# Half of the output weights split in the output phase, and two of the gated attention's four token factors made from the other two

## The reference

```
b = cumsum(log_a) within a chunk of 64 tokens
b_last = b[last of chunk];  b_ref = b[middle of chunk]
att = (q * exp(b - b_ref)) @ (k * exp(b_ref - b)).T, causal within the chunk
o_intra = att @ v
q_inter = q * exp(b)
k_state = k * exp(b_last - b)
decay   = exp(b_last)
for each chunk: o_inter = q_inter @ state; state = decay * state + k_state.T @ v
o = rms_norm(o_intra + o_inter) * silu(gate)
x = x + concat([o, cross_attention]) @ w_out
```

## Time and profile before

| what | value |
|---|---|
| median of 3 runs | 2726.78 us (2722.53 to 2730.62) |
| the profiled execution: its time | 2718.5 us |
| the profiled execution: its span | 2716.7 us |
| mean granted clock of TensorE | 0.979 |
| busy: PE, weight loads, DVE, ACT, POOL | 96%, 81%, 49%, 31%, 7% |
| `gla_phase` | 220 to 424 us of the span |
| first output phase | 427 to 548 us of the span |

### The profile page before, as it was taken

How to read it: one execution, slowest core, us unless ns; L and a number is a source line. 1 busy time by engine, 2 the same in 40 slices (tenths; PEclk the granted TensorE clock), 3 DMA queues, 4 the chain that set the end, 5 groups by cost and what they waited for, 6 DMA issues and landing times. The chain is left out here.

```text
span 2716.7 us, 33074 instructions
## 1 busy us (share of the span) xinstructions
PE 2596.6 (96%) x12444; PEld 2201.7 (81%) x12444; DVE 1325.9 (49%) x2306; ACT 847.0 (31%) x1774; POOL 202.8 (7%) x271
## 2 busy tenths in 40 slices
PE   7998878999999999998999999997999999999999
PEld 7996767878888888887888888787778888888887
DVE  4423572444454445546544562453645444554445
ACT  6434442332222222224325433324332222222221
POOL 1100140000000000001211111111000000000000
PEclk9999978999999999998999999998999999999999
DMA  4320301031111111102102001102421111111111
GB/s 145 88 70 20 109 1 47 32 95 47 47 48 53 46 46 47 54 31 101 47 16 75 32 32 51 59 16 86 148 72 55 47 61 47 46 54 47 46 39 62
DMA packets 165246, 153.88 MB, mean 57 GB/s; under 512 B 32857, under 2 KB 135497, under 8 KB 165129
## 3 DMA queue, kind: packets, MB, share of 16 engines
q1 hardware_dynamic: 160968, 152.31, 17.6%
q10 hardware_dynamic: 4160, 0.02, 0.1%
HBM read 134.69 MB, written 17.61 MB: 56 GB/s over the span
## 5 line engine op out<-in xcount | busy, mean ns | idle before, releaser
L356 PE MATMUL psum<-hT_hi,f_up_hi 128*128 128x512 f32 x1376 | 426.8, 389 | 4.5 <-PEq L562 3.9
L356 PE MATMUL psum<-hT_hi,f_up_lo 128*128 128x512 f32 x1376 | 426.2, 389 | 0.0
L356 PE MATMUL psum<-hT_lo,f_up_hi 128*128 128x512 f32 x1376 | 426.2, 389 | 0.0
L238 DVE TENSOR_TENSOR f_up_lo<-raw,f_up_hi 128x1024 fp32r<-128x1024 f32 x84 | 102.9, 1225 | 489.8 <-ACT f_up_hi L182 489.8
L356 PEld LDWEIGHTS psum<-hT_hi,f_up_hi 128*128 128x128 f32 x1376 | 258.1, 188 | 59.3 <-issue 5.9
L356 PEld LDWEIGHTS psum<-hT_hi,f_up_lo 128*128 128x128 f32 x1376 | 258.3, 188 | 53.7
L356 PEld LDWEIGHTS psum<-hT_lo,f_up_hi 128*128 128x128 f32 x1376 | 258.3, 188 | 53.5
L256 DVE TENSOR_TENSOR XY<-XY,psum 128x512 f32<-128x512 f32 x352 | 234.4, 684 | 113.9 <-PE psum L52 113.7
L182 ACT ACTIVATE f_up_hi<-raw 128x1024 fp32r<-128x1024 f32 x84 | 89.1, 1061 | 614.5 <-PE psum L356 589.0
L50 PE MATMUL psum<-w_hi,hT_hi 128*128 128x512 f32 (+1 forms) x640 | 249.9, 391 | 17.0 <-DVE w_lo L805 10.5
L50 PE MATMUL psum<-f_down_hi,f_act_hi 128*128 128x512 f32 x640 | 249.0, 389 | 0.0
(11 more groups left out here) (296 smaller groups left out, 4046.3 us busy)
## 6 DMA issues: line engine op xcount, KB each, us to landing
raw<-in_ffn_w_up_dram SPq DMA_DIRECT2D x88, 512.0 KB, 3.8
f_down_raw<-in_ffn_w_down_dram SPq DMA_DIRECT2D x22, 1024.0 KB, 4.9
w_raw<-in_b_w_in_dram SPq DMA_DIRECT2D x18, 1024.0 KB, 5.4
w_raw<-in_a_w_in_dram SPq DMA_DIRECT2D x8, 768.0 KB, 5.9
group_out<-stage SPq DMA_DIRECT2D x24, 256.0 KB, 2.2
o_outs<-group_out SPq DMA_DIRECT2D x24, 256.0 KB, 3.4
XY<-in_x_dram SPq DMA_DIRECT2D x8, 512.0 KB, 10.5
w_raw<-in_xa_w_kv_dram SPq DMA_DIRECT2D x8, 512.0 KB, 3.6
```

The costliest lines, as they stand in the source:

```text
L238: nc.vector.tensor_tensor(up_lo[n_slot][:, :, :], up_raw[n_slot], up_hi[n_slot][:, :, :].bitcast(F32), ALU.subtract).then_inc(up_split, 1)
L356: mm = nc.tensor.matmul(psum[:, 2 * j + half, :], w[j][:, d, :], h[:, d, half * HALF:(half + 1) * HALF], start=first, stop=final)
```

## The change

Two things are changed.

- `k_out` and `q_in` are no longer exponentials of their own. The small values exp(b at the chunk's middle), exp(b at its end) and exp(end minus middle), 96 x 16 each, are made on ScalarE behind `q_mid` in `factor`. VectorE then makes `k_out` as `k_mid` (already times k) times exp(end minus middle), and `q_in` as `q_mid` times exp(middle). ScalarE's exponentials of 96 x 1024 go from four to two a head; VectorE's subtraction L1699 shrinks to 96 x 16, and its copy L1707 goes. Waits follow: `k_out` and `q_in` wait for the other two products, for the small values and for TensorE's reads of the head before.
- GpSimd splits four chunks of the output weights instead of eight: 0 and 1 after head 1, 2 and 3 after head 3's mask. Chunks 4 to 7 are split in `out_phase`, the high parts by ScalarE after `y_part(0)`, the low parts by VectorE after its `y_part(0)`. The staging buffer stays live until then. The cross attention's two small tables move into `rank_rows`, which is free by then.

Diff, cut to its core:

```diff
@@ -502,14 +502,17 @@
     def wait_loaded(self, eng, k):
         eng.wait_ge(self.raws.loaded[k % 2], self.before[k % 2] + 16 * (k // 2 + 1))
+    def raw(self, k):
+        return self.stage[:, k, :] if self.stage is not None else self.raws.tiles[k % 2][:, :]
     def high_part(self, act, k):
-        self.wait_loaded(act, k)
-        self.nc.scalar.activation(self.hi[:, k, :], self.raws.tiles[k % 2][:, :], ACT.Copy).then_inc(self.high, 1)
+        if self.stage is None:
+            self.wait_loaded(act, k)
+        self.nc.scalar.activation(self.hi[:, k, :], self.raw(k), ACT.Copy).then_inc(self.high, 1)
     def low_part(self, dve, k):
         dve.wait_ge(self.high, k + 1)
-        self.nc.vector.tensor_tensor(self.lo[:, k, :], self.raws.tiles[k % 2][:, :], self.hi[:, k, :].bitcast(F32),
-                                     ALU.subtract).then_inc(self.split, 1)
+        self.nc.vector.tensor_tensor(self.lo[:, k, :], self.raw(k), self.hi[:, k, :].bitcast(F32), ALU.subtract).then_inc(self.split, 1)
     def load_ahead(self, sp, k):
...
@@ -519,7 +522,7 @@
-        self.nc, self.chunks, self.w, self.ahead, self.hi, self.lo, self.stage = nc, DC, w_out, DC, hi, lo, stage
+        self.nc, self.chunks, self.w, self.ahead, self.hi, self.lo, self.stage = nc, DC, w_out, DC // 2, hi, lo, stage
...
@@ -587,7 +590,7 @@
-            for k in range(weights.ahead + 2, chunks - 1 if merge else chunks):
+            for k in range(weights.ahead + 2, (chunks - 1 if merge else chunks) if weights.stage is None else 0):
...
@@ class CrossUnits, __init__ @@
-    def __init__(self, nc, ctx, ph, psum, ident, q_of, keys, vals, out_of, room, banks, out_bank):
-
+    def __init__(self, nc, ctx, ph, psum, ident, q_of, keys, vals, out_of, room, sums, banks, out_bank):
-        self.neg_top, self.total = sb("neg_top"), sb("total")
+        self.neg_top, self.total = sums[:, 0:2 * self.PAIRS], sums[:, 2 * self.PAIRS:4 * self.PAIRS]
...
@@ gla_phase @@
-        from_mid, to_last = soft, z
+        from_mid = soft
+        ends = sb("ends", [DK, 4, CH])
+        to_mid, mid_to_last, to_last = (ends[:, i, :] for i in range(3))
-        chunk_decay = sb("chunk_decay", [DK, CH])
+        chunk_decay = ends[:, 3, :]
+        ended = sem("ended")
-                           lambda t, i: Y[:, t, D_MIX + i * 2 * XA_DIM:D_MIX + (i + 1) * 2 * XA_DIM], cross_room + [V[:, 0:4, 0:P]], ((0, 1), 3), lambda u: bank(cross_of[u]))
+                           lambda t, i: Y[:, t, D_MIX + i * 2 * XA_DIM:D_MIX + (i + 1) * 2 * XA_DIM], cross_room + [V[:, 0:4, 0:P]], rank_rows[:, :, :].rearrange("p t r -> p (t r)"), ((0, 1), 3), lambda u: bank(cross_of[u]))
-        SPLITS = {(1, "rstd"): range(0, 2), (2, "mask"): range(2, 4), (2, "rstd"): range(4, 6), (3, "mask"): range(6, 8)}
+        SPLITS = {(1, "rstd"): range(0, 2), (3, "mask"): range(2, 4)}
+            for i in range(out_weights.chunks // 2):
+                sp.wait_ge(out_weights.pairs_loaded[i], 16)
...
-                    act.wait_ge(timed, 4 * h - (i if h > 1 else 0))
+                    act.wait_ge(timed, 4 * h - 3 + i)
             def gate_in(h):
-                    act.wait_ge(expd, 4 * h)
+                    act.wait_ge(expd, 2 * h)
+                    act.wait_ge(shifted, h)
             def factor(h, i):
-                out, src, s, entries = ((q_mid, from_mid, 1, ("cross",)), (k_mid, from_mid, -1, ("cross",)), (k_out, to_last, 1, ("delta",)), (q_in, cum, 1, ("out", 4)))[i]
+                out, sign = ((q_mid, 1), (k_mid, -1))[i]
-                    act.wait_ge(mixed, mixes_before(at(h - 1, *entries)))
-                nc.scalar.activation(out[:, :], src[:, :], ACT.Exp, scale=s / 16.0).then_inc(expd, 1)
+                    act.wait_ge(timed, 4 * h)
+                    act.wait_ge(mixed, mixes_before(at(h - 1, "cross")))
+                nc.scalar.activation(out[:, :], from_mid[:, :], ACT.Exp, scale=sign / 16.0).then_inc(expd, 1)
+                if i == 0:
+                    if h:
+                        act.wait_ge(factored, h)
+                    c = cum.rearrange("p (c i) -> p c i", i=CHUNK)
+                    nc.scalar.activation(to_mid, c[:, :, CHUNK // 2 - 1], ACT.Exp, scale=1.0 / 16.0)
+                    nc.scalar.activation(chunk_decay, c[:, :, CHUNK - 1], ACT.Exp, scale=1.0 / 16.0)
+                    nc.scalar.activation(mid_to_last, to_last, ACT.Exp, scale=1.0 / 16.0).then_inc(ended, 1)
...
-            for i in range(4):
+            for i in range(2):
-                if more:
-                    factor(h + 1, 2)
-                if more:
-                    factor(h + 1, 3)
...
-                mid, last = (c[:, :, i:i + 1].broadcast_to([DK, CH, CHUNK]) for i in (CHUNK // 2 - 1, CHUNK - 1))
-                nc.vector.tensor_tensor(from_mid.rearrange("p (c i) -> p c i", i=CHUNK), c, mid, ALU.subtract)
-                nc.vector.tensor_tensor(to_last.rearrange("p (c i) -> p c i", i=CHUNK), last, c, ALU.subtract).then_inc(shifted, 1)
+                mid, last = (c[:, :, i:i + 1] for i in (CHUNK // 2 - 1, CHUNK - 1))
+                if h:
+                    dve.wait_ge(ended, h)
+                nc.vector.tensor_tensor(to_last.unsqueeze(2), last, mid, ALU.subtract)
+                nc.vector.tensor_tensor(from_mid.rearrange("p (c i) -> p c i", i=CHUNK), c, mid.broadcast_to([DK, CH, CHUNK]), ALU.subtract).then_inc(shifted, 1)
             def product(h, i):
-                x, part = ((q_mid, 0), (k_mid, 1), (k_out, 1), (q_in, 0))[i]
-                src = source(h, part)
-                dve.wait_ge(expd, 4 * h + i + 1)
-                if i == 3:
-                    chain(nc.vector.tensor_copy(chunk_decay[:, :], q_in[:, :].rearrange("p (c i) -> p c i", i=CHUNK)[:, :, CHUNK - 1]))
-                    cd = chunk_decay[:, :].rearrange("p (c two) -> p c two", two=2)
+                if i < 2:
+                    x = (q_mid, k_mid)[i][:, :].rearrange("p (c n) -> p c n", n=P)
+                    src = source(h, i)
+                    dve.wait_ge(expd, 2 * h + i + 1)
+                    if h == LAST:
+                        dve.wait_ge(gathered, 32)
+                    else:
+                        dve.wait_ge(copied, 2 * h + 1 + i)
+                    if i == 0:
+                        nc.vector.scalar_tensor_tensor(x, src, float(DK) ** -0.5, x, ALU.mult, ALU.mult).then_inc(timed, 1)
+                    else:
+                        nc.vector.tensor_tensor(x, src, x, ALU.mult).then_inc(timed, 1)
+                    return
+                x, out, end = ((k_mid, k_out, mid_to_last), (q_mid, q_in, to_mid))[i - 2]
+                if i == 2:
+                    dve.wait_ge(ended, h + 1)
+                    if h:
+                        dve.wait_ge(mixed, mixes_before(at(h - 1, "delta")))
+                        dve.wait_ge(state_ready, (PAIRS - 1) * h)
+                    cd = chunk_decay.rearrange("p (c two) -> p c two", two=2)
                     nc.vector.tensor_tensor(decay[:, :], cd[:, :, 0], cd[:, :, 1], ALU.mult)
-                x = x[:, :].rearrange("p (c n) -> p c n", n=P)
-                if h == LAST:
-                    dve.wait_ge(gathered, 32)
-                else:
-                    dve.wait_ge(copied, 2 * h + 1 + part)
-                if part == 0:
-                    nc.vector.scalar_tensor_tensor(x, src, float(DK) ** -0.5, x, ALU.mult, ALU.mult).then_inc(timed, 1)
-                else:
-                    nc.vector.tensor_tensor(x, src, x, ALU.mult).then_inc(timed, 1)
+                elif h:
+                    dve.wait_ge(mixed, mixes_before(at(h - 1, "out", 4)))
+                dve.wait_ge(timed, 4 * h + 2)
+                nc.vector.tensor_tensor(out[:, :].rearrange("p (c i) -> p c i", i=CHUNK), x[:, :].rearrange("p (c i) -> p c i", i=CHUNK),
+                                        end.unsqueeze(2).broadcast_to([DK, CH, CHUNK]), ALU.mult).then_inc(timed, 1)
             def cross_pair(h):
-                cd = chunk_decay[:, :].rearrange("p (c two) -> p c two", two=2)
+                cd = chunk_decay.rearrange("p (c two) -> p c two", two=2)
...
-            product(0, 3)
+            product(0, 3)
             def token_products(h):
-                pe.wait_ge(timed, 4 * h + (4 if h == 0 else 2))
+                pe.wait_ge(timed, 4 * h + 2)
```

4 lines of the change are left out of this document (1 added, 3 removed).

## The result

| | before | after |
|---|---|---|
| median of the timed runs | 2725.92 us (2722.53 to 2730.62, 5 runs) | 2707.9 us (2706.48 to 2710.32, 5 runs) |
| ratio to before | | 0.9931, 95% interval [0.992, 0.9942] |
| the profiled execution: its time, span | 2718.5, 2716.7 us | 2706.76, 2704.9 us |
| mean granted clock | 0.979 | 0.980 |

The account below looks back on a forecast made before the run. TensorE, busy 96% of the span, was the bound, so only its idle times and low-clock stretches could give. 3.8 + 0.2 + 8.2 + 5.1 + 0.4 = 17.7 us, carried to the median: 2709.1 us, range 2702 to 2719.

Parts of the forecast that it names:

- head 0, chain: Start of head 0: smaller subtraction and fewer large exponentials take 2.35 us off TensorE's 2.93 us wait.
- head 0, clock: The 24 matmuls behind head 0's shortened gap run at the full clock, 1.5 us less.
- head 2, first gap, wait: Ahead of head 2's states: VectorE's lines return to medians, 4.0 us, and smaller L1699 gives 1.06; 5.1 us.
- behind it, clock less waits that stay: Three cross steps behind head 2's first gap return to the full clock: 3.1 us, with nothing as other bound.
- head 2, second gap: Two products fall to 1.22 us and a 1.00 us copy goes: 5.1 us off TensorE's 9.34 us wait.
- output phase: Start of output phase: earlier norm's gain saves 0.7 us, late x_old costs 0.3; net gain 0.4 us.
- the 0.3 us by which the low end of the gain is lowered: Allowance taken off the 13.1 us gain at the low end of the predicted range.
- of under 2 us: Second TensorE idle time said to remain amid head 2's cross steps, for VectorE's copy of the turned probabilities.
- list of four idle times: TensorE waits named in the gated attention: 2.93, 1.87 (again in head 1), 5.92 and 9.34 us.
- the clock does not come back: Rival: gaps shrink but what is left still lowers TensorE's clock; gain 13.1 us, 2713.7 us; chance 0.14.
- if the clock dips behind the short gaps: One of the signs that would show the forecast wrong: lower TensorE clock behind the shortened gaps.
- rival on the slow side: Late first x_old load delays all eight output-phase additions by 3.4 us: 9.5 us slower, 2736.3 us; chance 0.02.

Follow-up runs that it names:

- the repeats: Nothing edited: the kernel before once more, 2725.85 us (ratio 1.0006); the changed kernel twice more, 2704.46 us (0.9931) and 2707.5 us (0.9926).
- mask pair back: Changed kernel with one pair of weight splits put back on GpSimd behind head 2's mask: 2712.88 us, ratio 0.9957.
- splits only: Kernel before with only the weight splits moved, the four old factors and products kept: 2712.67 us, ratio 0.9958.
- experiment 9: Changed kernel with VectorE's two late products for the next head put between the second and third softmax step: 2699.97 us, again 2697.02 us.

## Why the prediction was right, point by point

| step of the sum | forecast | measured |
|---|---|---|
| head 0, chain | 2.35 | 2.58 (2.93 to 0.35) |
| head 0, clock | 1.5 | offset of the two traces behind it 3.94 in all: 1.4 |
| head 1 | 0.2 | 0.21 (6.11 to 5.90) |
| head 2, first gap, wait | 5.1 | 5.18 (5.92 to 0.74); between the repeats 4.14 |
| behind it, clock less waits that stay | 3.1 | 1.5; between the repeats 3.3 |
| head 2, second gap | 5.1 | 5.13 (9.34 to 4.21) |
| output phase | +0.7 and -0.3 | +1.28 and about -0.2 (first product to second addition, 13.50 and 13.68) |

*The waits.* The steps that are waits come to 13.15 us forecast (2.35, 0.2, 5.1, 5.1, 0.4). Measured in idle time they are 12.8 (2.58 + 0.21 + 5.18 - 1.56 + 5.13 + 1.28) between the first profiles and 11.6 between the repeats. What slowed VectorE was GpSimd, as argued, and lengths taken from the same lines in other heads gave the new gaps to 0.1 us. Two sizes were off. The three small exponentials, put at 0.6 us, held ScalarE for 0.34: an instruction's length is not its price in a queue, which is the distance between two starts. I had used that distance for the large ones and not for the small. No run shows the 0.3 us by which the low end of the gain is lowered; the three came out 0.26 us cheaper than my 0.6. By the Trainium skill (ScalarE: Activation LUTs, What ACT_TABLE_LOAD costs) an ACTIVATE with immediate scale and bias takes 186 ns and 0.833 ns an element, and ACTIVATEs back to back overlap by about 93 ns; for 16 elements I estimate 0.20 us each and 0.11 from start to start, and the rows agree. And I had counted with a second idle time "of under 2 us" in the cross steps. It was not in the trace: the matmuls at the low clock covered VectorE's copy. With the clock up TensorE is there first and waits 1.56 us; in the two kernels where it was low there (mask pair back, splits only) it waits 0.39 and 0.20. From the first gap's end to the second's start the kernels took 18.34 and 16.87 us (357.83 to 376.17, 353.39 to 370.26), 1.5 us apart: 3.0 of clock less 1.56. So between the first profiles the term "I take all 3.1 us" was too large by that wait, and 8.2 us for the gap measured 6.7, or 7.5 between the repeats (18.56 and 15.22 us). The list of four idle times also leaves out head 1's wait of 6.11 us, the second longest; experiment 9 found the next gain there.

*The clock.* I gave it 4.6 us, 1.5 and 3.1, each behind one gap. These two are near what the traces show there, and the rival "the clock does not come back" is wrong for head 0 (1.00 behind the gap) and half right in the first profile of after for head 2 (0.80), not in its repeat (1.00). By the prediction's own sign, "if the clock dips behind the short gaps", that first profile spoke against it. But I treated it as a property of a place. It is a matter of the execution too: 15.9 and 23.4 us of low clock in two profiles of one kernel. Timed medians of the changed kernel lie 18.0 to 20.3 us below those of before, against some 12 us of waiting, so by difference about 6 to 8 are clock, not 4.6. The sum is near because the waits were put a little high and the clock low, and that is luck in part: between the two profiled executions the gain was 11.7 us where the sum says 17.7, as their low clock differs by 0.5.

*The carry to the median.* I added 8.3 us to a profiled execution that was 7.4 us under its kernel's later median. That took the whole offset as if it stayed; the profile of after lay only 1.1 under its own. It was right to carry the gain and not the time, since nearly all the waits are the same in every execution.

*The output phase.* Four chunks are hidden, as costed, and eight would not be. The gain load came in at 2.2 us and gave all of the 1.3 that I had halved. That x_old is late and costs next to nothing stands too: loading it first gained nothing. The rival on the slow side needed the delay handed on from tile to tile, and it stops at the second addition. With eight chunks in the output phase it is handed on once, as TensorE's wait of 1.38 us.

## What to carry to other kernels

Where TensorE waits for VectorE, compare that engine's instructions with the same lines elsewhere in the program before anything else: here, those that took twice their median beside GpSimd were waiting for the end of its instruction, and they paid that wait whatever their size, so move the rival work, or count instructions instead of columns. Price a gap by its wait and, apart from that, by the clock of the stretch behind it, and take the second from several profiles. Before work is moved into a phase that has room, list the loads that stand behind it on its queue: four chunks cost nothing here, eight cost 3.3 us, with 2.8 us of waiting, half of it through a load.

## What the runs showed that I had not expected

- Stretches at the lower clock (0.50, that is 1.2 GHz) that begin while TensorE is busy without a pause, as in 292 to 300 in the first profile of after. That one is absent in both repeats and stands at the same place in three other kernels.
- Behind one and the same wait of 5.9 us in head 1, a granted clock over 16 us of 0.89 in one execution and 0.56 in another. What a wait costs in clock cannot be read from one profile.
- Subtractions of 8 and 16 columns on VectorE that take 2.09 and 2.14 us beside a GpSimd subtraction, and end within 0.03 us of its end.
- A load of 4 KB that lands in 2.2 us alone and in 4.4 beside loads of 512 KB, and so moved TensorE's first wait of the output phase by 1.28 us.
